# A two-block network on one core: modulation in shift-scale pairs, regrouped matmuls, output transposed early

## The reference

```
y = x * rsqrt(mean(x * x, -1) + 1e-5) * final_norm_g
```

## Time and profile before

| | before |
|---|---|
| median of 3 runs | 2740.63 us |
| the profiled execution | 2736.4 us |
| its span, first to last instruction | 2734.3 us |
| granted TensorE clock, mean | 0.979 |
| first matmul of the first projection | 123.77 us |
| last matmul of the last projection starts | 2712.02 us |
| busy: PE, DVE, ACT, POOL | 96%, 72%, 44%, 4% |

### The profile page before, as it was taken

The page is one execution under the profiler, slowest core; times in us unless marked ns, Lnnn a source line. Parts: engine busy times, 40 slices in busy tenths (PEclk is TensorE's granted clock), DMA queues, the critical chain, the costliest instruction groups (busy, mean ns, idle before and its releaser), DMA issues.

```text
span 2734.3 us, 39467 instructions
## 1 busy us (share of the span) xinstructions
PE 2613.2 (96%) x14629; PEld 2275.3 (83%) x14629; DVE 1957.0 (72%) x2772; ACT 1210.3 (44%) x1559; POOL 101.5 (4%) x145
## 2 busy tenths in 40 slices
PE   3499999999998999999999999998999999999998
PEld 2488888888887888888888888886888888888886
DVE  6977778887788888855666657997776644566554
ACT  1244653444554655544555541004554433444443
POOL 0011111100001000000000000000000000000000
PEclk8599999999999999999999999999999999999998
DMA  8798778865777777755666554552656655666553
GB/s 324 293 303 259 218 245 244 245 205 159 225 251 243 230 250 245 236 185 187 187 187 184 186 161 147 152 150 67 205 180 191 188 189 185 186 186 189 185 188 113
DMA packets 492579, 557.31 MB, mean 204 GB/s; under 512 B 18854, under 2 KB 458279, under 8 KB 492199
## 3 DMA queue, kind: packets, MB, share of 16 engines
q1 hardware_dynamic: 474023, 488.50, 56.1%
q0 software_dynamic: 18432, 67.12, 8.2%
HBM read 553.45 MB, written 2.10 MB: 203 GB/s over the span
## 4 chain that ended last, share of the span: by engine, by line
PE 92%; DVE 4%; issue 2%; DMA 1%; ACT 1%; SPq 1%; DVEq 0%; POOL 0%; ACTq 0%
PE ps L1413 53%; PE ps L1414 27%; PE ps L1711 8%; DVE wlo L834 1%; DVE norm_rows L931 1%; PE ms L1474 1%; PE ms L1452 1%; PE ms L1736 1%; DMA att<-in_x 0%; DVE tCDE L931 0%; PE ms L1565 0%; SPq L387 0%; DMA att<-in_w_ada 0%; DVE norm_rows L873 0%; PE ms L1721 0%
## 5 line engine op out<-in xcount | busy, mean ns | idle before, releaser
L1413 PE MATMUL ps<-xhl,whi 128*128 128x512 f32 (+1 forms) x4368 | 1547.9, 399 | 23.0 <-DVE xhl L895 16.7
L834 DVE TENSOR_TENSOR wlo<-raw,whi 128x1024 fp32r<-128x1024 f32 x794 | 971.1, 1224 | 627.8 <-ACT whi L512 619.0
L512 ACT CAST whi<-raw 128x1024 fp32r<-128x1024 f32 x794 | 831.2, 1050 | 1143.5 <-PE ps L1414 1067.8
L1414 PE MATMUL ps<-xhl,wlo 128*128 128x256 f32 (+1 forms) x4368 | 1223.6, 280 | 0.0
L1413 PEld LDWEIGHTS ps<-xhl,whi 128*128 128x128 f32 (+1 forms) x4368 | 822.6, 188 | 224.2 <-issue 29.8
L1414 PEld LDWEIGHTS ps<-xhl,wlo 128*128 128x128 f32 (+1 forms) x4368 | 826.5, 189 | 3.0 <-issue 2.9
L1413 PE MATMUL ps<-ghl,whi 128*128 128x512 f32 x1024 | 359.6, 393 | 0.0
L1414 PE MATMUL ps<-ghl,wlo 128*128 128x256 f32 x1024 | 289.6, 283 | 0.0
L1413 PE MATMUL ps<-fhl,whi 128*128 128x512 f32 x704 | 247.3, 394 | 0.0
L1413 PEld LDWEIGHTS ps<-ghl,whi 128*128 128x128 f32 x1024 | 192.3, 188 | 44.4
L1711 PE MATMUL ps<-xg,raw 128*128 128x256 f32 x1024 | 221.3, 379 | 0.0
(11 more groups left out here) (230 smaller groups left out, 1527.1 us busy)
## 6 DMA issues: line engine op xcount, KB each, us to landing
raw<-in_w_in SPq DMA_DIRECT2D x176, 512.0 KB, 4.3
raw<-in_w_up SPq DMA_DIRECT2D x176, 512.0 KB, 3.9
ada<-in_w_ada POOLq DMA_DIRECT2D x128, 512.0 KB, 4.7
raw<-in_ffn_w_up SPq DMA_DIRECT2D x128, 512.0 KB, 3.7
raw<-in_ffn_w_down SPq DMA_DIRECT2D x128, 512.0 KB, 3.4
raw<-in_conv_w_pw SPq DMA_DIRECT2D x96, 512.0 KB, 3.6
raw<-in_w_down SPq DMA_DIRECT2D x88, 512.0 KB, 3.4
att<-in_w_ada SPq DMA_DIRECT2D x32, 1024.0 KB, 6.9
```

What stands on the lines that cost most here:

```text
L512: nc.scalar.copy(whi[t % SPL][:, :, :], raw[t % RAW][:, :, :]).then_inc(s_hi, 1)
L834: nc.vector.tensor_tensor(wlo[t % SPL][:, :, :], raw[t % RAW][:, :, :], whi[t % SPL][:, :, :].bitcast(F32), ALU.subtract).then_inc(s_lo, 1)
L1413: mm(o, h, x, start=start, stop=stop, skip_group_check=True)
L1414: return mm(o[:, 0, :], l, x[:, 0, :], start=False, stop=stop, skip_group_check=True)
```

## The change

1. **Order of the modulation groups** (`FIRST`): a shift group, then the scale group of the same 512 features. After each two, DVE normalises and splits four chunks of x (`norm_first`), and PE multiplies the piece of the first projection that needs them (`first_unit`, at groups 3, 5 and 7; the fourth after group 7).
2. **c as weights for a quarter of it**: of each group's 16 chunks, 4 go to PE, with one column of c as the weights and the 128 x 512 tile moving (`first_rows`); ACT copies the row out (`row_out`), and PE adds it in with the sums of the 12 products left to DVE (`first_modulation`, now 3 matmuls a block instead of 2).
3. **Loads**: SP issues three vectors and then the modulation's weights, with pieces 0 to 3 behind groups 1 to 4; constants, x, positions and the other 19 vectors go out on ACT's queue.
4. **Angles** for the rotary embedding move from the opening into the projection's background work (`angles`, steps 4 to 12).
5. **`unit`**: of each chunk the two 512-column matmuls come first, then the two 256-column ones. The products are the same.
6. **The end**: in the last projection ACT multiplies each finished pair of chunks by the gain, PE turns it after the fifth unit of the next group, ACT copies it to `turned_out`. After the last unit the sums of squares are taken per row (one column out), the root is made on 128 x 2, and eight 128 x 512 pieces are scaled in place, five by DVE and three by ACT, and stored.

```
+FIRST = [j + 4 * half for j in range(4) for half in range(2)]
+BY_TENSOR = 4
+BY_VECTOR = DC - BY_TENSOR
+B_ANGLE = 4
...
-        first_sum = [mod_sum, [tCDE[:, 0:NCOL], tCDE[:, NCOL:2 * NCOL]]]
+        first_sum = [[ch(26, 28), ch(28, 30)], [tCDE[:, 0:NCOL], tCDE[:, NCOL:2 * NCOL]]]
...
+            load_vectors(sp, first_vecs, s_vin[0])
...
+            for n, first in enumerate(FIRST):
                 for q in range(4):
-                    sp.wait_ge(s_chain, g * DC + 4 * (q + 1))
-                    sp.dma_start(ada_first[q][:, :, :], w_ada[q][:, :, bass.ds(g * NCOL, NCOL)]).then_inc(s_adaring[q], 16)
+                    if n and q == 0:
+                        sp.wait_ge(s_firstmm, n)
+                    elif n:
+                        sp.wait_ge(s_first, BY_VECTOR * (n - 1) + 4 * q)
+                    sp.dma_start(ada_first[q][:, :, :], w_ada[q][:, :, first * NCOL:(first + 1) * NCOL]).then_inc(s_adaring[q], 16)
+                if 1 <= n <= SPL:
+                    sp.dma_start(raw[n - 1][:, :, :], w_in[n - 1][:, :, 0:CW]).then_inc(s_land[n - 1], 16)
...
+            act.dma_start(cons[:, :], A["consts"]).then_inc(s_in[0], 16)
+            x_in = A["x"].rearrange("b (c p) (h t) -> p (b c) h t", p=P, t=T)
+            for c in range(2):
+                act.dma_start(att[:, 8 * c:8 * c + 8, :], x_in[:, c]).then_inc(s_in[2], 16)
+            act.dma_start(posi, A["positions"]).then_inc(s_in[1], 16)
+            load_vectors(act, other_vecs, s_vin[1])
...
+            row_out(0)
             for b in range(DC // 2):
...
             for i in range(DC // 2):
                 act.wait_ge(s_trx, i + 1)
                 square(i, i)
-            act.wait_ge(s_ang, 1)
-            for n in range(2):
-                nc.scalar.activation(rope[:, 2 * n, :], rB[:, T * n:T * (n + 1)], ACT.Sin).then_inc(s_sin, 1)
-                nc.scalar.activation(rope[:, 2 * n + 1, :], rA[:, T * n:T * (n + 1)], ACT.Sin).then_inc(s_sin, 1)
-            for t in range(SPL):
-                split_hi(0, t)
+            row_out(1)
+            for b in range(2):
+                act.wait_ge(s_tr, 9 + b + 1)
+                lo = P + 4 * P * b
+                nc.scalar.copy(cols[:, lo:lo + 4 * P], (bank_z, bank_f)[(9 + b) % 2]).then_inc(s_trc, 1)
+            split_hi(0, 0)
+            row_out(2)
             root(0)
-            norm_hi(0, lambda c: mod[:, c:c + 1])
+            first_hi(0)
+            split_hi(0, 1)
+            row_out(3)
+            row_out(4)
+            first_hi(1)
+            split_hi(0, 2)
+            row_out(5)
+            split_hi(0, 3)
+            row_out(6)
+            first_hi(2)
+            row_out(7)
+            first_hi(3)
...
+            def gained_out(j):
+                if j:
+                    act.wait_ge(s_ft, j)
+                for m in range(PC):
+                    ins = nc.scalar.activation(tmp2[:, m, :], res[:, 2 * j + m, :], ACT.Copy, scale=col("final_norm_g_2", 2 * j + m))
+                ins.then_inc(s_fin, 1)
+            def turned_copy(j):
+                act.wait_ge(s_ft, j + 1)
+                nc.scalar.copy(turned_out[:, :, CW * j:CW * (j + 1)], (bank_z, bank_f)[j % 2].rearrange("p (h n) -> p h n", h=2)).then_inc(s_fc, 1)
...
-            root(6)
-            for b in range(8):
-                act.wait_ge(s_ft, b + 1)
-                nc.scalar.copy(ucv[:, 2 * b:2 * b + 2, :].rearrange("p a t -> p (a t)"), out_banks[b % 4]).then_inc(s_fc, 1)
+            gained_out(7)
+            nc.scalar.activation(warm[:, 6:7], one_c[:, 0:1], ACT.Sqrt)
+            act.wait_ge(s_var, 7)
+            nc.scalar.activation(rstd[:, 0:2], varr[:, 0:2], ACT.Sqrt).then_inc(s_std, 1)
+            turned_copy(7)
+            act.wait_ge(s_fr, 1)
...
+            def first_products(n):
+                dve.wait_ge(s_gemv, n + 1)
+                for i in range(BY_VECTOR):
+                    kc = BY_TENSOR + i
+                    if i % 4 == 0:
+                        dve.wait_ge(s_adaring[kc // 4], 16 * (n + 1))
+                    sums, cx = first_sum[n % 2][i % 2], cact[:, kc:kc + 1]
+                    w = ada_first[kc // 4][:, kc % 4, :]
+                    if i < 2:
+                        nc.vector.tensor_scalar(sums, w, cx, None, ALU.mult).then_inc(s_first, 1)
+                    else:
+                        dve.wait_ge(s_first, BY_VECTOR * n + i - 1)
+                        nc.vector.scalar_tensor_tensor(sums, w, cx, sums, ALU.mult, ALU.add).then_inc(s_first, 1)
+            def read_first(n):
+                a = FIRST[n]
+                c = slice(4 * a, 4 * a + 4)
+                dve.wait_ge(s_gemv, 2 + n + 1)
+                nc.vector.tensor_tensor(mod[:, c], first_bank[n % 2][:, c], cols[:, AT["b_ada"] + 4 * a:AT["b_ada"] + 4 * a + 4], ALU.add).then_inc(s_firstmod, 1)
...
+            def norm_first(j):
+                c0 = 4 * j
+                dve.wait_ge(s_firstmod, 2 * j + 2)
+                sv.did(nc.vector.scalar_tensor_tensor(gmod[:, 0, c0:c0 + 4], mod[:, DC + c0:DC + c0 + 4], 1.0, cols[:, AT["g_mix"] + c0:AT["g_mix"] + c0 + 4],
+                                                      ALU.add, ALU.mult))
+                sv.wait()
+                if j:
+                    dve.wait_ge(s_h, c0)
+                for c in range(c0, c0 + 4):
+                    nc.vector.scalar_tensor_tensor(sq[:, c % 4, :], res[:, c, :], gmod[:, 0, c:c + 1], rstd[:, :], ALU.mult, ALU.mult).then_inc(s_nt, 1)
+                for c in range(c0, c0 + 4):
+                    dve.wait_ge(s_nt, c + 1)
+                    dve.wait_ge(s_nh, c + 1)
+                    nc.vector.scalar_tensor_tensor(xl[:, c, :], sq[:, c % 4, :], mod[:, c:c + 1], xh[:, c, :].bitcast(F32),
+                                                   ALU.add, ALU.subtract).then_inc(s_h, 1)
...
+            for n in range(ADA_START):
+                first_products(n)
+                if n == 0:
+                    dve.wait_ge(s_in[1], 16)
+                    nc.vector.tensor_copy(posf, posi).then_inc(s_posf, 1)
+                if n:
+                    read_first(n - 1)
+                if n == 2:
+                    root(0, EPS1, s_acc, 8)
+                if n and n % 2 == 0:
+                    norm_first(n // 2 - 1)
+                if n >= 2 and n < 6:
+                    split_lo(0, n - 2)
+            read_first(ADA_START - 1)
+            norm_first(3)
+            dve.sem_inc(s_chain, DC * (1 + ADA_START))
...
-            root(6, EPS2, s_var2, 5)
-            for c in range(DC):
-                nc.vector.scalar_tensor_tensor(res[:, c, :], res[:, c, :], col("final_norm_g_2", c), rstd[:, :], ALU.mult, ALU.mult).then_inc(s_fin, 1)
+            dve.wait_ge(s_var2, 5)
+            few = slice(0, 2)
+            nc.vector.tensor_scalar(varr[:, few], bank_o[:, few], 1.0 / D, EPS2, ALU.mult, ALU.add).then_inc(s_var, 1)
...
+            for h, p in by_vector:
+                if p == 3:
+                    dve.wait_ge(s_fc, 8)
+                nc.vector.tensor_scalar(out_rows(h, p), out_rows(h, p), rstd[:, h:h + 1], None, ALU.mult).then_inc(s_fv, 1)
...
                     for m in range(PC):
-                        w = slice(m * P, (m + 1) * P)
-                        ins = products(o[:, m, :, :], whi[t % SPL][:, c, w], wlo[t % SPL][:, c, w], x, first and c == 0, last and c == KC - 1)
+                        mm(o[:, m, :, :], whi[t % SPL][:, c, m * P:(m + 1) * P], x, start=first and c == 0, stop=last and c == KC - 1, skip_group_check=True)
+                    for m in range(PC):
+                        ins = mm(o[:, m, 0, :], wlo[t % SPL][:, c, m * P:(m + 1) * P], x[:, 0, :], start=False, stop=last and c == KC - 1, skip_group_check=True)
                 ins.then_inc(s_used, 1)
...
+            def first_rows(n):
+                pe.wait_ge(s_adaring[0], 16 * (n + 1))
+                if n:
+                    pe.wait_ge(s_row, n)
+                for kc in range(BY_TENSOR):
+                    ins = mm(bank_row, cact[:, kc:kc + 1], ada_first[0][:, kc, :], start=kc == 0, stop=kc == BY_TENSOR - 1)
+                ins.then_inc(s_firstmm, 1)
+            def first_modulation(n):
+                bank, a = first_bank[n % 2], 4 * FIRST[n]
+                if n >= 2:
+                    pe.wait_ge(s_firstmod, n - 1)
+                pe.wait_ge(s_first, BY_VECTOR * (n + 1))
+                pe.wait_ge(s_row, n + 1)
+                for m in range(4):
+                    w = slice(P * m, P * (m + 1))
+                    for i, x in enumerate(first_sum[n % 2]):
+                        mm(bank[:, a + m:a + m + 1], x[:, w], ones[:, 0:1], start=i == 0, stop=False)
+                    ins = mm(bank[:, a + m:a + m + 1], row[:, w], ones[0:1, 0:1], start=False, stop=True)
+                ins.then_inc(s_gemv, 1)
...
+            turned(0, [att[:, 16, 0:P]])
+            pe.wait_ge(s_cact, 1)
+            pe.wait_ge(s_const, 3)
+            first_rows(0)
+            pe.wait_ge(s_in[2], 32)
```

(54 more changed lines are left out.)

235 lines of the change are left out of this document (117 added, 118 removed).

## The result

Five runs of the change have a median of 2724.89 us (2723.85 to 2730.76), five of the kernel before on the same chip 2740.63 us; the ratio is 0.9944, 95% interval 0.993 to 0.9959. The forecast was 2731.0, range 2685 to 2751, faster at 0.65. The profiled execution took 2724.74 us, with a span of 2722.9.

What follows compares the result with a forecast made beforehand. PE, busy 96% of the span, was taken as the bound in the projections; -1.6 (opening) - 2 (pairs) - 6.5 (end) = -10.1 on the profiled 2736.4 us gave 2726.3, with 4.2 us to the median 2730.5, stated as 2731, range 2685 to 2751.

Steps and rivals of the forecast that it cites:

- opening: Start of the program up to PE's fifth unit: it would start at 136 us against 137.64, a gain of 1.6 us.
- pairs: High and low matmul pairs in the projections, 6,336 of them at 0.350 us: new order gives -2 us, ends -32 and +13.
- end: Behind the last projection matmul: 12 us instead of 22.0, less 3.5 us for added transposes, a gain of 6.5 us.
- the middle of the two: Pair pace under the new order, between ends of -5 and +2 ns: taken as 0.3 ns less, or -2 us.
- it goes with the columns that stream: Pairs: pace is set by streamed columns, which stay, not by weight load length or change of bank.
- The first rival: Pairs get faster: fewer long-short changes give up to 15 ns a pair, 95 us, 2638; or 2701 at pace 0.345; chance 0.27.
- the limit that the prediction named for itself: Pairs: the prediction called itself wrong if the pair's time moves by more than 2 ns.
- PE's hold on the first quarters: Opening: PE's late row products delay first-quarter loads by about 1.2 us a group for five groups, 114 to 120 us.
- POOL's load: Opening, before piece 4's low half: DVE's background products need a load issued only then, 4.7 us to landing, 5.2 with wake-up.
- a PE with 14 to 30 us of work in 23 has few waits: Opening: PE's work per two groups against DVE's 23 us; the reason for placing 136 nearer the free end.
- the rival with PE as the bound: First modulation: PE at half clock needs 29.7 us per two groups against DVE's 23; fifth unit at 152, kernel 2748.5; chance 0.12.
- point of decision: Opening: PE bounds the first modulation once it spends more than 56% of its work at half clock.

Runs made afterwards that it cites:

- 5: Kernel before with the new matmul order in a unit and the new end, but the old opening: 2723.13 us, ratio 0.9925.
- 11: The change itself measured once more, unedited: 2728.83 us, ratio 0.9964 to the kernel before.
- 1: Kernel before with only the new order in a unit (512-column matmuls first, then the 256-column ones): 2726.10 us, ratio 0.9952.
- run 2: The change with the unit's old order (512, 256, 512, 256 columns) put back: 2741.75 us, ratio 1.0007 to the kernel before.

## Why the prediction was right in sign and sum, and wrong in its parts

| term | forecast | measured |
|---|---|---|
| opening | -1.6 | +4.0 in the first trace, +6 in the mean of three; +5 to +11 by the ratios of 5, change and 11 |
| pairs | -2 (ends -32 and +13) | -13.2 (ratio of 1); 2.0 ns a pair |
| end | -6.5 (-10.0 and +3.5) | -7.4 (ratios); -9.0 and +3.1 in the traces |
| sum | -10.1 | -15.3 and -9.9 (ratios of the change and of 11) |

*Pairs.* The bounds held; the value between them was the step that failed: "Nothing in the rows says which; I take the middle of the two, 0.3 ns less". The middle of its own ends, -5 and +2 ns, is not 0.3 but 1.5 ns less, 348.5 ns a pair, or 9.5 us; taken rightly, the term would have been near the measured one and the forecast 2723.5. The rows had the paces by counts, 0.345 and 0.352, which swept 346.7, 351.1 and 353.3 into two; weighted by how long each lasts they gave 350.3, and the new single pace lies 2.0 under it. Since opening and end together brought nothing in run 2 (1.0007), this term is nearly the whole measured gain. The argument that a matmul owes nothing to its neighbour ("it goes with the columns that stream") is wrong: with the same columns and the same number of matmuls, five orders gave paces from 346.7 to 353.3 ns. The first rival had the sign but not the size: it wanted 580 pairs or more in the 200 us from 1300 on and the forecast 568, and 576 came; in the mean the pair moved by 2.0 ns, just the limit that the prediction named for itself. The Trainium skill (TensorE: Matmul & The Clock Gate, section "Back-to-back issue gap") would give an estimated 325 ns a pair in every order, and no run here comes nearer than 346.7.

*Opening.* Up to the row products of group 1 each time was right within 1.5 us: c at 13.4 (13; the 23 DMA issues come to 12.0 us by the row that it used, not 11, and took 11.3), row products at 19.5 (19), transposes at 24.6 (26), group 1 at 41.3 (40), DVE's group 2 at 57.0 (55.5). Then DVE took 67.5 us to the last products where 58.5 and 6 were forecast, 124.5 instead of 120; PE's hold on the first quarters was sized at 1.2 us a group, 6 us in all; by difference it was 9, and DVE's waits for weights in this stretch add up to 10.3. The norm ended at 132.4 (127.5), POOL's load cost what it should (3.7 us of wait), and the fifth unit started at 138.71 instead of 136. The step that failed here is "a PE with 14 to 30 us of work in 23 has few waits": the mechanism was near that of the rival with PE as the bound, at a mixed clock instead of a half one and with DVE and PE waiting in turn, and it lost 5 to 11 us of that rival's 14.4. The prediction's point of decision, 56% of PE's work at half clock, was near: a mean clock of 0.73 between 1.00 and 0.50 puts 54% of the stretch at the lower one.

*End.* Right within 1.1 us in each part: 13.0 us for 12, 3.1 for 3.5.

So 2731 was near because two errors of opposite sign, +7 to +12 us in the opening and -11 in the pairs, nearly cancelled; that was luck. A range that held the result says little about its terms: only the runs of single parts told that the opening as it was built should have been left out.

## What to carry to other kernels

Before work is moved from a busy engine to an idle one, look at what the idle one will then release: here the products that PE took held back DMA issues for all of the next group, and the saving of 2.7 us a group on DVE turned into 27.7 us of waits. When each matmul costs more than its columns should, try a few orders of the same matmuls; it is an edit of a few lines, 0.5% here, and bounds read from the old order held the new pace here without telling where between them it lies. Time each part of a combined change by itself: a sum that comes out right hides what should be dropped.

## What the runs showed of the hardware

- The same 512- and 256-column float32r matmuls, with the same weights, banks and operands, took 348.3 ns a pair in twos and 350.8 to 351.1 in fours; in turn it depended on the stretch of the program and in part on the execution, 346.7 to 353.3. Which bank a short matmul goes to made no difference in the time (2712.60 us against 2712.40 in twos; in turn the mean with `xhl` was 350.2 ns both ways).
- More work on PE bought clock: row products twice, and the granted clock between 50 and 125 us rose from 0.74 to 0.89, which gave back a part of the added time.
- A busy PE lost its clock. In the change it had hardly any idle time between 25.1 and 53 us, doing sums over partitions (one column out), sums of squares and row products, and the granted clock still fell in the middle of it, from full (2.4 GHz) to half. Windows of the change:

```profile
40.00:45.00 5.00, 5.00 (x30) 3.39 (x28) 0.00 (x0) 2.59 (x4) 0.00 (x0) 1.00 0.49 145
45.00:50.00 5.00, 5.00 (x14) 2.04 (x14) 0.80 (x3) 0.00 (x0) 0.00 (x0) 0.56 1.05 403
```

The passes of the row products show it: start to start 0.43 us in group 1 (37.81 us), 0.85 in group 2 (46.57). The forecast had 3.4 and 6.9 us for eight at the two levels, near the 3.59 and 6.47 us that they took; what it lacked is that being busy does not by itself hold the clock. In this trace the fall came during the sums over partitions (42.9 to 46.6 us). From group 3 on the passes go from 0.85 to 0.43 us within each group's row products (the first time at 66.2 us), so each time the clock rose again while PE made row products.
